# An MLP in 512-column blocks with the sample tokens taken out: one core, a two-layer decoder step

## The reference, cut to what matters

```
h = relu(rmsnorm(x, norm_ffn[l]) @ w_up[l])        # w_up: 1024 x 4096
x = x + (h * h) @ w_down[l]                        # w_down: 4096 x 1024
```

## Time and profile before

| | us |
|---|---|
| median of 3 runs | 2502.69 |
| lowest, highest | 2500.77, 2505.36 |
| the profiled execution's own time | 2495.87 |
| span of its trace | 2496.7 |

### The profile page before, as it was taken

One profiled execution on the slowest core, in us unless ns is written; L12 is line 12 of the kernel. 1 busy time (PEld: TensorE's weight loads), 2 busy tenths in 40 slices (PEclk: granted clock), 3 DMA queues, 4 the chain that ended last, 5 costly groups with the idle time before them and its releaser, 6 DMA issues.

```text
span 2496.7 us, 36951 instructions
## 1 busy us (share of the span) xinstructions
PE 2415.8 (97%) x15530; PEld 2310.6 (93%) x15530; DVE 1172.6 (47%) x2055; ACT 655.3 (26%) x1096; POOL 162.5 (7%) x208
## 2 busy tenths in 40 slices
PE   6999999989999999999999999999999999999997
PEld 6899898878999999999999877878999999999997
DVE  6555555567433333333346675476434334334333
ACT  3233222334211111111213453353212112112113
POOL 3000000003000000000002010022000000000002
PEclk7999999999999999999999999999999999999999
DMA  3111121111111111111112311101111111111111
GB/s 107 49 44 57 47 65 38 44 36 43 43 43 51 44 43 51 44 43 51 43 43 62 94 34 41 34 18 40 46 51 43 43 51 43 43 51 43 43 51 70
DMA packets 177416, 120.55 MB, mean 48 GB/s; under 512 B 23623, under 2 KB 173044, under 8 KB 177220
## 3 DMA queue, kind: packets, MB, share of 16 engines
q1 hardware_dynamic: 177108, 118.10, 16.2%
q10 hardware_dynamic: 144, 0.02, 0.0%
HBM read 110.94 MB, written 12.33 MB: 49 GB/s over the span
## 4 chain that ended last, share of the span: by engine, by line
PE 73%; issue 19%; DVE 4%; POOL 2%; ACT 1%; DMA 1%; SPq 0%; POOLq 0%; ACTq 0%; DVEq 0%
PE acc L1606 59%; PE acc L1888 3%; PE acc L1890 3%; PE acc L1889 3%; PE acc L1907 2%; PE acc L1930 1%; PE acc L1918 1%; POOL small L991 1%; DVE rstd L1054 1%; DVE w_lo L1036 1%; DVE x_res L1193 0%; DMA out_y_prompt<-y_out 0%; DVE q_t L1441 0%; DVE prob L1475 0%; POOL small L989 0%
## 5 line engine op out<-in xcount | busy, mean ns | idle before, releaser
L1067 DVE TENSOR_TENSOR x_res<-x_res,acc 128x1056 f32<-128x1056 f32 x128 | 160.4, 1253 | 413.4 <-PE acc L1606 413.4
L1606 PE MATMUL acc<-x_hi,w_hi 128*128 128x352 f32 x1560 | 341.1, 327 | 13.4 <-DVE x_lo L1042 5.6
L688 ACT ACTIVATE w_hi<-w_raw 128x1024 fp32r<-128x1024 f32 x180 | 189.2, 1051 | 614.9 <-PE acc L1606 527.6
L1606 PE MATMUL acc<-x_hi,w_lo 128*128 128x352 f32 x1560 | 337.5, 324 | 0.0
L1606 PE MATMUL acc<-x_lo,w_hi 128*128 128x352 f32 x1560 | 337.4, 324 | 0.0
L1606 PE MATMUL acc<-h_hi,w_hi 128*128 128x352 f32 x1536 | 332.1, 324 | 0.0
L1606 PE MATMUL acc<-h_hi,w_lo 128*128 128x352 f32 x1536 | 331.1, 323 | 0.0
L1606 PE MATMUL acc<-h_lo,w_hi 128*128 128x352 f32 x1536 | 330.6, 323 | 0.0
L1606 PEld LDWEIGHTS acc<-x_hi,w_hi 128*128 128x128 f32 x1560 | 267.2, 190 | 16.8 <-issue 11.5
L1606 PEld LDWEIGHTS acc<-x_hi,w_lo 128*128 128x128 f32 x1560 | 268.9, 189 | 0.0
L1606 PEld LDWEIGHTS acc<-x_lo,w_hi 128*128 128x128 f32 x1560 | 266.4, 189 | 0.0
(11 more groups left out here) (265 smaller groups left out, 3085.8 us busy)
## 6 DMA issues: line engine op xcount, KB each, us to landing
w_raw<-in_w_up SPq DMA_DIRECT2D x64, 512.0 KB
w_raw<-in_w_down SPq DMA_DIRECT2D x64, 512.0 KB
w_raw<-in_w_mlstm_in SPq DMA_DIRECT2D x24, 512.0 KB
x_in<-in_x_prompt SPq DMA_DIRECT2D x8, 512.0 KB, 3.9
w_raw<-in_w_mlstm_out SPq DMA_DIRECT2D x8, 512.0 KB
w_raw<-in_w_q SPq DMA_DIRECT2D x16, 256.0 KB
w_raw<-in_w_attn_out SPq DMA_DIRECT2D x16, 256.0 KB
out_y_prompt<-y_out SPq DMA_DIRECT2D x8, 512.0 KB, 2.6
```

The lines of the kernel that those rows point to most:

```text
L688: nc.scalar.activation(w_hi[:, s.parity], w_raw[:, s.parity], ACT.Copy).then_inc(hi_split, 1)
L1067: V.tensor_tensor(blocks(x_res[:, k]), blocks(x_res[:, k]), group(o), ALU.add).then_inc(out_taken, 1)
L1606: last = T.matmul(out[:, b], w[:, k, m], x[:, TN * b:TN * b + TN], start=(k == 0 and i == 0), stop=(k == k_chunks - 1 and i == 2))
```

## The change

The MLP's prompt tokens are computed in two blocks of 512 columns, two banks for a row. All chunks of inputs go into the first bank and then all into the second, with three matmuls for each chunk (high*high, high*low, low*high), so a slab is 48 matmuls of 512 columns and each is preceded by a load of different weights.

The 32 sample tokens leave these rows. They become stationary operands: `x_s` (128 inputs x 32 tokens) stands in the array and the unsplit fp32 weights `w_raw` stream past it. Four chunks of inputs use four 32-column tiles of the array at once, each tile writing its own 32 output partitions of one bank. An up slab adds 8 such matmuls of 128 columns (`sample_up`), a down slab 4 of 256 columns (`sample_down`, which accumulates in banks 6 and 7 through all 8 blocks). After the 4 up slabs of a block ACT copies the bank to `s_up`, and 4 matmuls against `eye4`, four identity matrices above each other, add the four tiles and turn the result to features by tokens (`sample_turn`); DVE scales, applies the ReLU and squares it into `h_s`. At the end of a layer `sample_out` does the same with 8 matmuls for the output, and DVE adds them to `x_res`.

`walk_mlp` writes up 1, down 0, up 2, down 1 out and leaves two trips of the loop. The ReLU of the prompt tokens moves from ACT to DVE: one instruction takes the maximum with 0 and multiplies. Transfers of MLP slabs wait for the sample matmuls on the slab two before (`s_done`) where they waited for its split (`lo_split`). In the last down block nothing of `x_res` is final until the sample tokens are added behind row 4. So ACT issues all eight `prepare` steps behind its last split, and DVE its own in groups behind rows 5, 6 and 7. The attention's first blocks use banks in another order.

```diff
     up(At(0), At(s), At(o), 0)
-    with eng.Fori(0, (NB - 2) // 2) as i:
...
+    up(At(1), At(s + 4), At(o + 4), 1)
+    down(At(0), At(s + 8), At(o + 8), 0)
+    up(At(2), At(s + 12), At(o + 16), 0)
+    down(At(1), At(s + 16), At(o + 20), 1)
+    with eng.Fori(0, (NB - 4) // 2) as i:
...
@@ ACT, down block
-                        for k in (2 * c, 2 * c + 1):
-                            if last and layer == 0:
+                        if last and c == 2:
+                            act.wait_ge(s_done, sample_count(s + 3).value)
+                            nc.scalar.activation(s_down[:, 1], acc[:, DOWN_BANK + 1, :], ACT.Copy).then_inc(sd_taken, 1)
+                    if last:
+                        for k in range(KD):
+                            if layer == 0:
                                 prepare(2, KV, k)
-                            elif last:
+                            else:
                                 final_gain(k)
@@ DVE
+                def rows_final(o, k):
+
+                    dve.wait_ge(out_taken, (o + (k + 1)).value)
+                    if k == 4:
+                        dve.wait_ge(sdt_ready, layer + 1)
+                        V.tensor_tensor(x_res[:, :, SEQ:], x_res[:, :, SEQ:],
+                                        acc[:, TURN_BANK[layer], 0:KD * SAMP].rearrange("p (k n) -> p k n", k=KD), ALU.add
+                                        ).then_inc(sdt_taken, 1)
...
+                    mark(x_final)
+                    if layer == 0:
+                        for k in ((), (0, 1), (2, 3), (4, 5, 6, 7))[k - 4]:
+                            prepare(2, KV, k)
...
-                        scaled(o + c, act_a[:])
-                        dve.wait_ge(relu_ready, (h + 1).value)
-                        V.tensor_tensor(act_a[:], act_a[:], act_b[:], ALU.mult).then_inc(act_ready, 1)
+                        dve.wait_ge(out_ready, (o + (c + 1)).value)
+                        V.tensor_tensor(halves(act_a[:, 0:SEQ]), group(o + c), halves(rstd[:, 0:SEQ]), ALU.mult).then_inc(out_taken, 1)
+                        dve.wait_ge(out_taken, (o + (c + 1)).value)
+                        V.scalar_tensor_tensor(act_a[:, 0:SEQ], act_a[:, 0:SEQ], 0.0, act_a[:, 0:SEQ], ALU.max, ALU.mult
+                                               ).then_inc(act_ready, 1)
@@ PE
-            def chunk(s, o, n, k, k_chunks, moving):
+            def row(s, o, n, k_chunks, moving, ready=None, between=None):
...
+                for b, k in [(b, k) for b in range(2) for k in range(k_chunks)]:
+                    if ready is not None and b == 0:
+                        ready(k)
+                    mh, ml = moving(k)
+                    for i, (w, x) in enumerate(((hi, mh), (hi, ml), (lo, mh))):
+                        last = T.matmul(out[:, b], w[:, k, m], x[:, 512 * b:512 * b + 512],
                                         start=(k == 0 and i == 0), stop=(k == k_chunks - 1 and i == 2))
...
+                def sample_up(f, s, c):
...
+                    for k in range(KD):
+                        tile = slice(SAMP * (k % 4), SAMP * (k % 4) + SAMP)
+                        x = T.matmul(acc[tile, UP_BANK[layer], P * c:P * c + P], x_s[:, k], weights[:, k],
+                                     start=(k < 4), stop=(k >= 4))
...
+                def sample_turn(f):
...
+                    for c in range(4):
+                        x = T.matmul(acc[:, TURN_BANK[layer], SAMP * c:SAMP * c + SAMP], s_up[:, P * c:P * c + P], eye4[:],
+                                     start=True, stop=True)
...
+                def sample_down(f, s, c, half):
...
+                    for k in range(4):
+                        tile = slice(SAMP * k, SAMP * k + SAMP)
+                        x = T.matmul(acc[tile, DOWN_BANK + c // 2, 256 * (c % 2):256 * (c % 2) + 256], h_s[:, half, k], weights[:, k],
+                                     start=is_block(f, 0) and c % 2 == 0, stop=is_block(f, NB - 1) and c % 2 == 1)
...
+                        pe.wait_ge(lo_split, (s + (c + 1)).value)
+                        if not first:
+                            sample_up(f, s + c, c)
```

More of the change, by code:

```diff
@@ L184, in walk_mlp, with is_block, sample_count @@
     down(At(NB - 1), At(s + 8), At(o + 12), 1)
+def is_block(f, n):
+    return f.index is None and f.const == n
+def sample_count(s):
+    return s + ((8 * NB - S_MLP1 if s.const >= S_MLP1 else -S_MLP0) + 1)
 def build(nc, io):
@@ L1664, in _ @@
             pe.wait_ge(xt_taken, NT)
-            slab(At(0), At(0), KD, normed, prepared(0), sum_squares(0))
+            pe.wait_ge(lo_split, 1)
+            hi, lo = (w[:, 0].rearrange("p (k m) -> p k m", k=KD) for w in (w_hi, w_lo))
+            for k in range(KD):
+                prepared(0)(k)
+                for b in range(TB):
+                    T.matmul(gates[:, b], hi[:, k], x_hi[:, k, span(b)], start=(k == 0), stop=False)
+                    T.matmul(gates[:, b], hi[:, k], x_lo[:, k, span(b)], start=False, stop=False)
+                    x = T.matmul(gates[:, b], lo[:, k], x_hi[:, k, span(b)], start=False, stop=(k == KD - 1))
+                if k == KD - 1:
+                    x.then_inc(out_ready, 1)
+                sum_squares(0)(k)
             def dense(chunks):
@@ L1841, in up, with sample_out @@
+                def sample_out():
+                    pe.wait_ge(sd_taken, 2 * layer + 2)
+                    pe.wait_ge(st_taken, fb + NB)
+                    for d in range(KD):
+                        x = T.matmul(acc[:, TURN_BANK[layer], SAMP * d:SAMP * d + SAMP],
+                                     s_down[:, d // 4, P * (d % 4):P * (d % 4) + P], eye4[:], start=True, stop=True)
+                    x.then_inc(sdt_ready, 1)
                 def up(f, s, o, half):
-                    first = f.index is None and f.const == 0
```

196 lines of the change are left out of this document (125 added, 71 removed).

## The result

The changed kernel takes **2559.76 us** (median of 4, 2557.04 to 2560.99) against 2502.34 for the kernel before, a ratio of 1.0227 (95% interval 1.0209 to 1.0244): **+57.4 us where +24.4 were forecast**. The direction was right and the time lies in the range, but the sum of the prediction is off by 33 us, and most of that is one term.

The account below looks back on a forecast made before the run. PE's own pace was taken to bound the kernel. Dense matmuls -94.6, sample matmuls +97, turning +17, layer 0's end +8, layer 1 +0.5, gains -3.5 gave +24.4 us on 2502.7: 2527 us, range 2475 to 2572.

Parts of the forecast that it names:

- What bounds the kernel: Whole kernel: PE's own pace decides; the MLP's 9216 matmuls at 161.6 ns make 1489.3 of 2496.7 us.
- The dense matmuls: MLP prompt rows: 6144 matmuls of 512 columns at 227 ns, a fixed extra of 13.5 ns each; -94.6 us.
- Rival 3: Dense MLP matmuls: the extra grows with the columns, 235 ns each, +73 us, 2576 us; chance 0.10.
- The break-even at 223 ns: Dense MLP matmuls: at 223.0 ns each, the kernels before and after the change take equal time.
- Rival 1: Dense MLP matmuls: a late weight load's extra vanishes at 512 columns, 216 ns, 2460 us (219 to 221: 2480 to 2490); chance 0.17.
- rival 5: MLP slabs: late transfers or sample steps holding DVE up make PE wait, 1 us a slab, 2655 us; chance 0.03.
- Sample matmuls and turning: MLP slab seams: 0.76 us for each of 128 slabs, +97 us; turning back to features by tokens, +17 us.
- rival 4: Sample matmuls: the four array tiles don't overlap, +1.28 us a slab, +164 us, 2690 us; chance 0.02.
- rival 2: Sample matmuls: entering and leaving the tiles costs nothing, 0.5 us a slab instead of 0.76, 2494 us; chance 0.08.
- The end of layer 0's MLP: Behind layer 0's last down block: PE waits 6.4 us for POOL's seven sums, then restarts at the lower clock; +8 us.
- What is gained besides: Both MLPs: ReLU on DVE starts row 2 earlier, -2 us; one loop seam fewer in each layer, -3.5 us together.
- Ahead of the MLP and at the end: Outside the MLPs: nothing forecast ahead; +0.5 us in layer 1, whose last chunk's square waits for row 7 as before.

Follow-up runs that it names:

- (1024; 0, 0): Changed kernel with dense rows reading from other places: chunks 1024 columns apart instead of 1056, high and low tensors unshifted; 226.8 ns a matmul at 512 columns.
- packed chunks: Changed kernel with the hidden activations' chunks 1024 columns apart instead of 1056, affecting down rows alone; 2541.81 us, ratio 1.0167.
- the quiet second pass: Changed kernel with layer 0's up rows inside the loop computed twice; the second pass, other engines and transfers silent, took 232.3 ns a matmul; whole kernel 2736 us.
- the first trace: Trace of the changed kernel's first measurement, 2559.76 us; the same kernel, unchanged, was run and traced a second time at 2554.37 us.

## Why the prediction was right or wrong

**What bounds the kernel: right.** Waits for other engines are 2.4 us of the two MLPs, and PE's pace decided.

**The dense matmuls: the step that failed.** The forecast was 6144 x 227 = 1394.7 us, -94.6; measured are 6144 x 232.0 = 1425.4, -65.5 against 9216 x 161.77. The step read "Taken as a fixed cost that gives 213.3 + 13.5", and gave as its reason that nothing is added at the lower clock. That reason says only that the extra hides behind slower columns; it doesn't say whether it is the same for every width and place. In the changed kernel's layout it is not: 12.5 ns at 352 columns and 18.8 at 512, so the term was 5 ns a matmul too small. The step had not asked where the columns lie. Where (1024; 0, 0) puts them the extra is 13.3 ns at 352 and 13.5 at 512, fixed as forecast, and 227 ns is what a matmul takes there (227.4 with packed chunks); 128 bytes further it is 11.6 and 19.9. At 352 columns the two places differ by 2 ns and the row of the K/V projection could not show it; at 512 they differ by 6. The number forecast exists, but not for this layout. Rival 3, the extra that grows with the columns, had 235 ns and a chance of 0.10; 232 lies nearer to it than to 227, and just outside the forecast's own 224 to 231, but its mechanism too holds for this layout only.

**The break-even at 223 ns** could not be reached: the best place found gives 226.8. Rival 1 (216 to 221) is ruled out: the load doesn't come late for want of time, and the quiet second pass shows that no neighbour holds the stream back. Nor did a wait decide (rival 5).

**Sample matmuls and turning: right.** 0.77 us for a down slab and for 56 of 58 up slabs, forecast 0.76 (the other two, 1.9 us, hold the waits for `w_lo`); 0.8 more for a turning, as forecast; 115.9 for 114 in all by the seams, 109 net by taking them out. Tiles overlap (rival 4 out), and entering and leaving them costs what the attention's rows said (rival 2 out).

**The end of layer 0's MLP: mechanism right, size wrong.** +12 to +15 us for +8. The term took 2.58 us for every sum from the row at 1342.12. DVE was not idle there. It was just ending an `x_lo`, and its next instruction came second and did the waiting (2.82 us where it takes 1.22 alone):

```profile
1342.96 2.82 DVE L1036 TENSOR_TENSOR w_lo<-w_raw,w_hi 128x1024 fp32r<-128x1024 f32 x1 [0.28 <-ACT w_hi L688]
```

In the changed kernel an `x_lo` is already under way or waiting when five of the seven sums begin, so the sums wait, and they take 3.3 to 3.4. That puts 4.4 us onto PE's wait, 12.4 in place of 8. PE restarts at the lower clock as forecast: from the sums' start to the next dense matmul 2.80 us, where two times 0.86 would be the full one.

**What is gained besides: -12 for -3.5.** This is what is left when the dense term (-65.5) and the seams (+115.9) are taken from the MLPs' +38.4. The traces account for it. Between dense matmuls that follow each other the kernel before has 42 gaps of over 200 ns in the MLPs, 13.5 us over the pitch: 4.9 in two waits for `w_lo` behind the first rows, 3.2 at the lower clock behind them, 4.4 at the turns of the loop, 1.0 at the sums. The changed kernel has four beyond its seams, 1.5 us: its two waits for `w_lo` are shorter and stand within the seams' sum, the clock doesn't fall behind them, and the turns of the loop no longer show. The forecast had counted one turn of the loop in each layer.

**Ahead of the MLP and at the end:** nothing and 0.5 forecast, +5.1 and +4.1 in the first trace, +3.4 and +1.5 in the second; in part stretches at the lower clock that move from run to run, in part open.

**The sum** by measured terms: -65.5 + 115.9 - 12.0 + 14.8 + 5.1 + 4.1 = +62.4, the difference of the spans.

## What to carry to other kernels

A time a matmul that was measured at one width and in one layout gives neither a fixed extra nor a rate a column: here each holds, in a layout of its own. Until the new width has been measured at the new addresses, the forecast has to carry both figures, and fewer, wider matmuls may be no gain at all. The changed kernel won 65 us on its dense matmuls, of which 9216 x 2.65 ns = 24 are the order of a row, which needed no other width, and paid 116 for the changes of shape. A duration for a GpSimd or VectorE instruction has to be taken from a row in which the other engine does what it will do in the new place, and in the same order: the one that comes second waits.

## What the runs showed of the hardware that was not expected

- The pitch of a split fp32 matmul of 512 columns goes from 226.8 to 236.7 ns with the first address of the moving columns alone: 128 bytes of shift cost 6 ns, one column of shift 10.
- With chunks 4224 bytes apart the extra over the columns rises in steps of about 3 ns: 12.2, 12.5, 15.6, 15.2, 16.0, 18.4, 18.8 ns for 256, 352, 384, 416, 448, 480, 512 columns. Where (1024; 0, 0) puts the columns it is 13.3 at 352 and 13.5 at 512; 128 bytes further 11.6 and 19.9.
- The pitch is the same, 232 ns, with DVE, ACT and DMA working and with all of them silent.
- POOL's sum and DVE's `x_lo`, 2.4 and 1.24 us alone, take 3.42 us as a pair when both are due, and the one that starts second is the longer for it.
